# RWKV and attention block: value rows of the last pair in quarters, gate projection over two steps, bias rows asked for at the last Y fill

## The reference

```python
def first_block(x, c, ...):
    mod = silu(c) @ w_ada + b_ada                  # shift, scale, gate
    h = rms_norm(x, norm_g) * (1 + scale) + shift
    proj = h @ w_in
    ps = token_shift(proj[..., :D_SHIFT], mu_shift)
    y_r, g_r = rwkv7_mix(ps, ...)                  # r, k, v, decay, a per head; then a norm per head
    q, ka, va, g_a = split(proj[..., D_SHIFT:], 4)
    y_a = chunk_band_attention(q, ka, va, q_norm_g, k_norm_g, rel_bias)
    y = concat([y_r * silu(g_r), y_a * silu(g_a)])
    return x + gate * (y @ w_out)

def chunk_band_attention(q, k, v, q_g, k_g, rel_bias):
    q, k = rms_norm(q, q_g), rms_norm(k, k_g)      # per head
    s = q @ k.T * HEAD_DIM ** -0.5 + bias          # bias: relative, by clipped distance
    return softmax(masked s) @ v
```

## Time and profile before

| | |
|---|---|
| three runs | 1452.07, 1447.54, 1445.89 us; median 1447.54 |
| profiled execution | 1450.88 us, its span 1449.1 us |
| busy share of the span | PE 89%, DVE 39%, ACT 24%, POOL 11% |
| mean granted clock of PE | 0.959 |
| HBM traffic | 299 MB read, 14 MB written |

### The profile page before, as it was taken

How to read it: one execution, slowest core, us unless ns; L and a number is a source line. 1 busy time by engine, 2 the same in 40 slices (tenths; PEclk the granted TensorE clock), 3 DMA queues, 4 the chain that set the end, 5 groups by cost and what they waited for, 6 DMA issues and landing times.

```text
span 1449.1 us, 21053 instructions
## 1 busy us (share of the span) xinstructions
PE 1297.0 (89%) x7518; PEld 644.0 (44%) x7519; DVE 567.5 (39%) x1074; ACT 346.1 (24%) x751; POOL 158.1 (11%) x276
## 2 busy tenths in 40 slices
PE   5989999999899999999999795799899878898786
PEld 2445656568854444644454344333333322333222
DVE  1356372745123333358786635212212211222124
ACT  1223232323134442212454421011101100101012
POOL 4011110201020000000000001211021111111110
PEclk9999999999999999999999896799999999999999
DMA  9250806142073110032110384189999999999994
GB/s 358 73 204 11 291 2 222 71 155 80 4 225 109 57 31 1 0 136 87 59 45 28 137 357 189 47 340 389 415 416 418 403 404 420 418 396 411 409 377 193
DMA packets 40047, 303.86 MB, mean 210 GB/s; under 512 B 7852, under 2 KB 8004, under 8 KB 22560
## 3 DMA queue, kind: packets, MB, share of 16 engines
q1 hardware_dynamic: 31520, 285.12, 50.0%
q0 software_dynamic: 8448, 17.67, 3.9%
HBM read 299.23 MB, written 13.75 MB: 216 GB/s over the span
## 4 chain that ended last, share of the span: by engine, by line
PE 68%; DMA 20%; DVE 5%; issue 3%; POOL 2%; ACT 2%; SPq 0%; DVEq 0%; ACTq 0%; POOLq 0%
PE bank L828 21%; DMA arena<-in_w_down 14%; PE bank L2769 9%; PE bank L759 8%; PE bank L2785 6%; PE bank L874 4%; DMA arena<-in_w_gu 3%; PE bank L837 2%; PE bank L817 2%; DMA arena<-in_ada_w 2%; PE bank L2759 1%; PE bank L1134 1%; DMA arena<-bias_scratch 1%; PE bank L1056 1%; PE bank L1072 1%
## 5 line engine op out<-in xcount | busy, mean ns | idle before, releaser
L828 PE MATMUL bank<-hT,arena 128*128 128x512 f32 x768 | 342.9, 602 | 0.0
L2769 PE MATMUL bank<-arena,hT 128*64 128x512 f32 x1024 | 231.6, 600 | 29.1 <-DMA arena<-in_w_gu 27.5
L828 PEld LDWEIGHTS bank<-hT,arena 128*128 128x128 f32 x768 | 145.0, 192 | 175.2 <-issue 172.0
L2769 PEld LDWEIGHTS bank<-arena,hT 128*64 128x64 f32 x1024 | 71.3, 137 | 167.7 <-issue 136.1
L2785 PE MATMUL bank<-arena,yT 128*64 128x512 f32 x512 | 125.9, 637 | 15.8 <-DMA arena<-in_w_down 15.8
L759 PE MATMUL bank<-arena,yT 128*128 128x512 f32 x256 | 115.6, 606 | 2.3 <-DVE yT L1629 2.3
L2929 DVE TENSOR_SCALAR hT<-hT 128x256 f32<-128x256 f32 x32 | 9.4, 294 | 250.9 <-ACT hT L2880 250.9
L759 PEld LDWEIGHTS bank<-arena,yT 128*128 128x128 f32 x256 | 48.7, 195 | 61.4 <-issue 57.1
L2785 PEld LDWEIGHTS bank<-arena,yT 128*64 128x64 f32 x512 | 36.0, 145 | 81.8 <-issue 62.7
L874 PEld LDWEIGHTS bank<-arena 64*64 64x64 f32 x1856 | 59.3, 135 | 27.9 <-issue 14.4
L2880 ACT ACTIVATE hT<-bank 128x256 f32<-128x256 f32 x32 | 12.3, 383 | 248.7 <-PE bank L2769 248.7
(11 more groups left out here) (476 smaller groups left out, 1581.6 us busy)
## 6 DMA issues: line engine op xcount, KB each, us to landing
arena<-in_w_gu SPq DMA_DIRECT2D x64, 2048.0 KB, 32.3
arena<-in_w_down SPq DMA_DIRECT2D x32, 2048.0 KB, 34.8
arena<-in_w_in SPq DMA_DIRECT2D x53, 512.0 KB, 4.7
arena<-in_ada_w SPq DMA_DIRECT2D x24, 1024.0 KB, 5.3
arena<-in_w_ada SPq DMA_DIRECT2D x8, 1024.0 KB, 9.3
arena<-in_w_out SPq DMA_DIRECT2D x8, 1024.0 KB, 15.2
arena<-in_w_ada SPq DMA_DIRECT2D x8, 512.0 KB, 5.7
arena<-expert_rows SPq DMA_DIRECT2D x4, 1024.0 KB, 7.9
```

What stands on the lines that cost most here:

```text
L828: last = T.matmul(bank[0:rows, :], w[:, k, 0:rows], hT[:, k, :], start=k == 0, stop=k == KD - 1)
L2769: last = T.matmul(banks[1 + ub][MT * h:MT * h + MT, :], tile.xT[:, k, :], wgu[u][:, k // 4, :, k % 4, 256 * h:256 * h + 256], start=k == 0 ...
```

## The change

In the last pair the value rows are no longer four blocks but 16 quarters (one token tile, 8 matmuls of 128 x 128 each, the four of a block in one bank). They stand: one ahead of W(1); two each after W(1) to W(4); one after W(5), W(6), and akv; one in each of the first three scan steps ahead of the wait for U's copy; one after the last Y fill. ADA_BANK joins the rotation for this pair, so the wait for the fifth modulation sum (`s_mod`, 5) moves from ahead of attention to ahead of the first quarter. The q and k projections of attention pair 0 go around the variance of the last pair; ACT copies the first of them to SBUF at once and squares it from there after its norm and the wait for `s_pair`. In attention the gate projection of pair p + 1 is begun at t = 2 (k 0 to 3) in a held bank and completed at t = 3 (k 4 to 7), where ACT now evicts it. POOL waits for the last Y fill in `filled` in place of `s_pair` ahead of the bias DMAs, and for `s_pair` only ahead of the gate row.

```diff
+            if not q:
+                free_banks[0].append(ADA_BANK)
+                plan_held(("va", 0))
             for l in range(1, LEVELS):
                 plan(("W", p, l), "act")
                 if l <= 4 and q:
                     plan_proj(q, PROJ_ORDER[l - 1])
-                if l <= 2 and not q:
-                    plan(("va", l - 1), "act")
+                if l in (2, 4) and not q:
+                    plan(("va", l // 2 - 1), "act")
+                    plan_held(("va", l // 2))
...
-                if t < 3:
-                    plan(("aproj", p + 1, t), "act")
+                    plan_held(("aproj", p + 1, 2))
+                if t != 2:
+                    plan(("aproj", p + 1, min(t, 2)), "act")
...
-            eng.wait_ge(s_pair, PAIRS)
+            eng.wait_ge(filled, fill_at[("Y", PAIRS - 1)] + 1)
             eng.wait_ge(s_biasst, 16)
             step = P // COPIES
             for b in range(step):
                 src = bass.AP(er_dram.tensor, 127 - b, [[ERL - step, COPIES], [COPIES * ERL, 8], [1, 512]])
                 eng.dma_start(bias[b::step, :, :], src).then_inc(s_biasld, 16)
+            eng.wait_ge(s_pair, PAIRS)
             eng.dma_start(gateB, bass.AP(mod_dram.tensor, 2 * DM, [[0, P], [1, DM]])).then_inc(s_gateB, 16)
...
+                def va_rows(count):
+                    for _ in range(0 if q else count):
+                        n, t = divmod(va_quarter[0], TT)
+                        va_quarter[0] += 1
+                        name = ("va", n)
+                        bank = fill(name) if t == TT - 1 else begin(name)
+                        w = chunk_ready(name)
+                        for k in range(KD):
+                            last = T.matmul(bank[:, CH(t)], hT[:, k, CH(t)], w[:, k, :], start=k == 0, stop=k == KD - 1)
+                        if t == TT - 1:
+                            full(last)
...
                 if p:
                     mean(p - 1)
+                if not q:
+                    eng.wait_ge(s_mod, 5)
                 ada_step()
+                va_rows(1)
...
                         pe_proj(("proj", q, PROJ_ORDER[l - 1]))
-                    elif l <= 2:
-                        pe_rows(("va", l - 1), hT)
-                    elif l == LEVELS - 2:
+                    elif q and l == LEVELS - 2:
                         ada_step()
+                    else:
+                        va_rows(2 if l <= 4 else 1)
...
                 full(out_chunk(TT - 1, fill(("Y", p))))
+                va_rows(1)
...
-            pe_rows(("va", 2), hT)
             mean(PAIRS - 1)
-            pe_rows(("va", 3), hT)
+            pe_proj(("aproj", 0, 0))
             variance(PAIRS - 1)
-            eng.wait_ge(s_mod, 5)
+            pe_proj(("aproj", 0, 1))
...
                     if t == 2:
                         qk_sums(p + 1)
-                    if t < 3:
+                        proj_part(("aproj", p + 1, 2), begin(("aproj", p + 1, 2)), range(0, 4))
+                    elif t < 2:
                         pe_proj(("aproj", p + 1, t))
+                    else:
+                        proj_part(("aproj", p + 1, 2), fill(("aproj", p + 1, 2)), range(4, KD))
...
+            va_out(3)
             act_sigmoid(("gate", PAIRS - 1), (t_g, None))
-            va_out(2)
             out_square(PAIRS - 1)
-            va_out(3)
-            out_norm(PAIRS - 1)
-            eng.wait_ge(s_pair, PAIRS)
...
+            bank = take(S, ("aproj", 0, 0))
+            empty(S, "act", S.activation(aq[:, 0, :], bank[:, :], ACT.Copy), ("aproj", 0, 0))
+            out_norm(PAIRS - 1)
+            eng.wait_ge(s_pair, PAIRS)
+            act.done(S.activation(asq[:, 0, :], aq[:, 0, :], ACT.Square))
+            eng.sem_inc(s_asq, 1)
+            aproj_out(0, 1)
...
-                    if t < 3:
-                        aproj_out(p + 1, t)
+                    if t != 2:
+                        aproj_out(p + 1, min(t, 2))
```

More of the change, by code:

```diff
@@ L214, in build_program @@
             plan(("akv", p), "act")
+            if not q:
+                plan(("va", 2), "act")
             plan(("TaT", p), "act")
+            if not q:
+                plan_held(("va", 3))
             for c in range(TT):
@@ L220, in build_program @@
             plan(("Y", p), "act")
-        plan(("va", 2), "act")
+        plan(("va", 3), "act")
         plan(("mean", PAIRS - 1), "dve")
-        plan(("va", 3), "act")
+        plan(("aproj", 0, 0), "act")
         plan(("var", PAIRS - 1), "act")
+        plan(("aproj", 0, 1), "act")
         free_banks[0] = list(range(8))
@@ L235, in plan_scores @@
                 plan(("score", p, t, h), "dve")
-        for j in range(2):
-            plan(("aproj", 0, j), "act")
         plan_held(("aproj", 0, 2))
@@ L367, in begin @@
             n = fill_at[name]
-            old, by = fills[bank_before[n]]
-            T.wait_ge(emptied[by], given[by][old])
+            if bank_before[n] is not None:
+                old, by = fills[bank_before[n]]
+                T.wait_ge(emptied[by], given[by][old])
             return banks[bank_of[n]]
@@ L926, in pe_block1 @@
                 q = p + 1 if p + 1 < PAIRS else None
-                ada_k = [0]
+                ada_k, va_quarter = [0], [0]
+                def va_rows(count):
[9 more added lines that the diff above has]
+                            full(last)
                 def ada_step():
@@ L1036, in pe_block1 @@
                 full(out_chunk(TT - 1, fill(("Y", p))))
+                va_rows(1)
                 assert ada_k[0] == (KD if q else 0)
-            pe_rows(("va", 2), hT)
+                assert va_quarter[0] == (0 if q else TT * TT)
             mean(PAIRS - 1)
-            pe_rows(("va", 3), hT)
+            pe_proj(("aproj", 0, 0))
             variance(PAIRS - 1)
-            eng.wait_ge(s_mod, 5)
+            pe_proj(("aproj", 0, 1))
             def qk_sums(p):
@@ L1106, in pe_block1 @@
             FIRST_K, LAST_K = range(KD - 1), (KD - 1,)
-            for j in range(2):
-                pe_proj(("aproj", 0, j))
             bank = begin(("aproj", 0, 2))
@@ L1256, in act_block1 @@
                         proj_raw(q, l - 1)
-                    if l <= 2 and not q:
-                        va_out(l - 1)
+                    if l in (2, 4) and not q:
+                        va_out(l // 2 - 1)
                     if l == 1:
@@ L1270, in act_block1 @@
                 empty(S, "act", S.activation(akv.rearrange("p c h i -> p (c h i)"), bank[:, :], ACT.Copy), ("akv", p))
+                if not q:
+                    va_out(2)
                 bank = take(S, ("TaT", p))
@@ L1321, in probs_exp @@
                     eng.sem_inc(s_pexp, 1)
-            for j in range(2):
-                aproj_out(0, j)
+            bank = take(S, ("aproj", 0, 0))
[5 more added lines that the diff above has]
+            aproj_out(0, 1)
             qk_norm(0)
```

## The result

Six runs of the changed kernel have a median of 1436.21 us (1433.03 to 1438.31); the runs of the kernel before, beside them and earlier, 1452.27 (1445.89 to 1454.45). The ratio is 0.991 with a 95% interval of 0.9892 to 0.9929. On the 1450.88 us of the profiled execution that is 13.1 us, between 10.3 and 15.7. The profiled execution of the changed kernel took 1438.31 us, with a span of 1436.6, 12.5 less than before. The 12.0 us that were forecast lie inside the interval.

What follows compares the result with a forecast made beforehand. PE's queue ahead of the DMA-bound expert stage was taken as the bound. Gains of 5.9 us (first scores), 3.4 (gate projection) and 2.7 (clock) sum to 12.0, giving a median of 1435.5 us, range 1430 to 1444.

Steps and rivals of the forecast that it cites:

- First quarter: Last RWKV pair, ahead of W(3,1): a 1.84 us quarter covers PE's 1.32 us wait; W(1) comes 0.3 us later.
- level waits: Last RWKV pair: quarters remove waits ahead of D blocks of levels 3 to 5 and DT(6), part of 3.4 us removed.
- last Y fill: End of the last RWKV pair's value work on PE: moves from 390.05 to 397.9 us.
- DVE in level 2: Last RWKV pair: DVE's last multiply could be late, slack under a microsecond; costed at 0, at most 1 us.
- The tie at the first scores: Head of attention: q/k norm needs 3.6 us after the sums against 3.60 of PE work; first scores at 424.1.
- POOL's new wait for the pair output: Ahead of gate row and memset: pair output at 412.6 us, earlier than the bias rows at 415.2, so no cost.
- The gate projection: Attention steps 2 and 3: splitting it replaces a 1.88 us wait by 0.7; gains 1.15 us three times, 3.4.
- The clock in attention: Attention pairs: both falls to half clock, each behind a 1.88 us idle, go; gains 2 x 1.37 = 2.7 us.
- Rival A: Attention: the clock falls stay, as idle isn't the whole condition; gain 9.3 us, 1438.2; chance 0.14.
- the last pair's clock: Last RWKV pair: granted clock 1.00 throughout despite waits of 0.43 to 1.32 us, taken as evidence for the clock term.
- The forecast of the median: Whole kernel: profiled 1450.88 less 12.0 gives 1438.9; the median lies 3.34 under the profiled one, so 1435.5 us.
- Rival C: Expert stage: its DMA rate drops, 1% costing 4.5 us; a 5% loss gives 1458 us; chance 0.08.

Runs made afterwards that it cites:

- whole blocks: Changed kernel with value rows as four whole blocks, one behind each of W(1) to W(4), no quarters elsewhere; ratio 0.9951 against the kernel before.
- gate-only kernel: Kernel before with only the gate projection split over attention steps 2 and 3; ratio 0.9961 against the kernel before.

## Why the prediction was right, point by point

**First quarter, level waits, last Y fill.** Right. The only waits left are the 0.76 and 0.43 us named, and the Y fill ended 67.95 us behind the transposes (396.26 in the chain), where 397.9 - 329.70 = 68.2 was forecast. DVE in level 2, whose slack I put under a microsecond, was done with its multiply at 350.48 and waited a microsecond for D(2).

**The tie at the first scores.** Right: 94.4 forecast, 94.21 measured, with a wait of 0.24 us for the norm. That the bias rows have to be asked for early, and that POOL's new wait for the pair output costs nothing, is borne out: the flag was up near 413.4, 7.6 us ahead of DVE's multiply, and the value rows alone, without that edit, made the kernel slower.

**The gate projection.** Right in mechanism and size, the replaced wait of 0.7 us included. The step got shorter by 1.08 us and not by 1.15. One term was missing: the transposes, O rows and scores behind a wait take 2.67 us (at full clock) and 2.41 without one. Three times 0.26, less three times 0.07, is the 0.6 us by which this stretch beat its forecast.

**The clock in attention.** Right in effect: no fall in pairs 0 to 2, in either execution. In the steps of pairs 0 to 2 in all executions, of 18 waits of 1.88 us 11 had a fall at their end or just behind; of 15 of 0.70 us none; of 3 of 2.4 us one; of 6 steps without a wait none. Ahead of the first scores, of four waits of 1.43 to 2.05 us one had. In the last attention pair, which the change leaves alone, waits of 0.70, 0.38 and 2.26 us follow each other closely, and there the clock fell in all 14 executions. The last of these waits in the changed kernel (timeline of PE):

```profile
541.18 8.83 PE L769 MATMUL bank<-arena,yT 128*128 128x512 f32 x16 [2.26 <-DVE yT L1663]
```

Rival A's premise (the idle isn't the whole condition) holds, its conclusion doesn't. The Trainium skill's section on psum-queue depth-cycling (TensorE: Matmul & The Clock Gate), weighed in the prediction, would have kept the falls; in attention they are gone.

**What failed** is the reading of the last pair's clock. I took its 1.00 as a property of the code, as evidence that short waits do no harm, and as no source of gain. It was one draw: with that code before and with whole blocks it fell in three of five executions, at 5.5 to 6.8 us a fall, and with the quarters in none of seven. So the sum of 12.0 us is right for the two profiled executions, where neither fell, and probably too small for the mean of many. The 10.7 us of values and bias rows together against the 6 expected point that way, and so does the spread: the ten executions of the gate-only kernel lie 12.7 us apart, the ten of the kernel with value rows only, which has the quarters, 5.4. The 13.1 us of the ratio don't settle it, as 12.0 lies in its interval. That the quarters prevent the fall rests on this count and not on a run that turns it on and off, and the mean share of it in the ratio isn't measured. The short waits of this pair may be the cause, as the Trainium skill's section just named has it, or the small matmuls of the scan, or both; no run tells them apart.

**Luck.** The forecast of the median, 1435.5 us, was met within 0.7. It started from the median of three executions of the kernel before, 1447.54; that of six is 4.7 us higher. And in the profiled executions the start gave 1.4 us that nobody had forecast, and the end took 1.8.

**The expert stage.** Rival C is out. From the first output rows to the end the 14 executions took 914 to 922 us, without a clear relation to how early they began. That scatter is larger than a single term of this change, and the -1.8 and +1.4 us of the first table are part of it and of the start's.

## What to carry to other kernels

Work that hides a wait should be cut to the size of the wait and dealt out over all of them: one or two quarters of 1.84 us over each wait of 0.75 us did what four blocks of 7.34 us could not. Before such a move, follow every other releaser of the same event; here a transfer asked for too late would have turned 6 us of gain into a loss, and moving it alone was worth 1.2 us of wait. And one profile's granted clock is a draw: look at a second execution before a stretch is called safe.

## What the runs showed of the hardware

In the last RWKV pair the granted clock stayed at 0.50 for 17 us in two executions and 14 us in a third, although PE was busy 15.24 of 16.00 us with small matmuls in one of these stretches, and it came back to 1.00 while the same small matmuls of the scan went on, with no bigger work between. The timeline of PE in the kernel with whole blocks shows it; like pairs of matmuls take 0.69 us at half clock and 0.39 at full clock:

```profile
392.76 0.69 PE L1039 MATMUL bank<-arena 128*128 128x64 f32 x2
...
398.75 0.39 PE L1039 MATMUL bank<-arena 128*128 128x64 f32 x2
...
404.64 1.13 PE L897 MATMUL bank<-arena,masks 128*128 128x512 f32 x2 [0.69 <-ACT arena L1299]
```

Eight DMAs of 256 KB from POOL's queue took 16.2 us to land in the changed kernel (396.56 to 412.8), all but the last two microseconds ahead of the output weights; 17.3 us with them before, and 21.8 us in the kernel with value rows only. So 5 MB of weights in their way cost them a microsecond or two when they were asked for 3.5 us later, and 5.6 when at the same time. Between 400 and 412.8 us of the changed kernel the 16 DMA engines were busy 99% or more while moving 208 to 225 GB/s, where the expert stage moves 392 GB/s at 96%.
